# Second layer of a two-block model on one core: where pairs of expert rows stand among the query columns and the head norms

## What is computed

```python
k, v = shared_kv(x)                       # 16 heads of 64, k is rms-normed per head
q = rmsnorm((h @ w_q).heads) * 64**-0.5   # the head norm of the query rows
z = q @ k.T                               # per block of 128 tokens, strictly causal
a = exp(log_sigmoid(z) + sums of -softplus(z) over the keys between)
x = x + g1 * ((a @ v) @ w_out)
h = modulate(rmsnorm(x))                  # then the expert layer:
s = (h @ w_q) against 2 x 128 sub-keys, 8 heads
expert = 16 best of the sums of the 16 best of each half, per head
act = gelu(<peer_u[expert], h>)           # 8 x 16 = 128 experts for each token
x = x + g2 * sum((softmax(scores) * act) * peer_v[expert])
```

## Time and profile before

| | |
|---|---|
| median of 3 runs | 2526.04 us (2524.95 to 2527.66) |
| the profiled execution, its own time | 2526.39 us |
| its span | 2524.7 us |
| PE busy | 2032.2 us (80%) |
| DVE busy | 1719.8 us (68%) |
| ACT busy | 955.0 us (38%) |
| POOL busy | 658.8 us (26%) |
| moved by DMA | 823.98 MB, of these 595.97 MB by POOL's gathers |

### The profile page before, as it was taken

The page is one execution under the profiler, slowest core; times in us unless marked ns, Lnnn a source line. Parts: engine busy times, 40 slices in busy tenths (PEclk is TensorE's granted clock), DMA queues, the critical chain, the costliest instruction groups (busy, mean ns, idle before and its releaser), DMA issues.

```text
span 2524.7 us, 33890 instructions
## 1 busy us (share of the span) xinstructions
PE 2032.2 (80%) x12150; PEld 1384.9 (55%) x12150; DVE 1719.8 (68%) x3454; ACT 955.0 (38%) x2101; POOL 658.8 (26%) x631
## 2 busy tenths in 40 slices
PE   8999999999999999997665587777577778556555
PEld 7999899899989979874321123243122325211111
DVE  5687787768778867677588555558754757776544
ACT  4434533444544345432332224423223732322222
POOL 0000001000000100024445433344432335444442
PEclk9999999999999999999887798899788889887767
DMA  7545577674547763279999999999999999999998
GB/s 304 212 167 209 182 277 283 240 262 161 202 172 277 268 256 142 84 319 388 422 421 422 419 423 422 403 421 421 412 404 401 421 410 383 421 422 421 422 421 337
DMA packets 110947, 823.98 MB, mean 326 GB/s; under 512 B 14432, under 2 KB 15344, under 8 KB 31040
## 3 DMA queue, kind: packets, MB, share of 16 engines
q0 software_dynamic: 90000, 595.97, 57.8%
q1 hardware_dynamic: 20784, 225.89, 23.3%
HBM read 820.76 MB, written 1.05 MB: 326 GB/s over the span
## 4 chain that ended last, share of the span: by engine, by line
PE 47%; DMA 27%; DVE 11%; ACT 5%; issue 4%; POOL 2%; DVEq 2%; ACTq 1%; SPq 0%; POOLq 0%
DMA ring_b<-in_peer_uv,eidx 17%; PE pd L647 14%; PE pa L647 10%; PE pr L1269 9%; PE pr L647 7%; DMA wring<-in_peer_uv,eidx 6%; DVE wring_r L1971 2%; DVE ring_b L2672 2%; DMA ring_c<-in_peer_uv,eidx 1%; DVE wring L2672 1%; PE pa L1387 1%; ACT junk L1719 1%; POOL ring_b L1915 1%; PE pd L1292 1%; PE pa L1292 1%
## 5 line engine op out<-in xcount | busy, mean ns | idle before, releaser
L1269 PE MATMUL pr<-ring_b,junk 128*64 128x512 f32 x880 | 288.6, 765 | 156.5 <-ACT junk L1719 155.8
L1269 PE MATMUL pr<-wring,junk 128*64 128x512 f32 x840 | 269.4, 748 | 171.1 <-ACT junk L1719 170.6
L1915 POOL DMA_INDIRECT ring_b<-in_peer_uv,eidx x220 | 252.9, 1150 | 532.8 <-PE pr L1269 302.4
L2672 DVE CUSTOM_DVE_ANT_0 ring_b<-ring_b,hrow 128x1024 f32<-128x1024 f32 x220 | 267.9, 1224 | 180.9 <-DMA ring_b<-in_peer_uv,eidx 174.2
L2672 DVE CUSTOM_DVE_ANT_0 wring<-wring,hrow 128x1024 f32<-128x1024 f32 x210 | 255.4, 1223 | 187.8 <-DMA wring<-in_peer_uv,eidx 181.7
L1915 POOL DMA_INDIRECT wring<-in_peer_uv,eidx x210 | 247.8, 1180 | 332.6 <-PE pr L1269 277.3
L1709 ACT ACTIVATE gel<-dots 128x2 f32<-128x2 f32 x255 | 51.8, 203 | 654.4 <-DVE dots L2672 650.7
L1899 POOL DMA_DIRECT2D aring<-in_ada_rows x112 | 60.2, 538 | 840.9 <-DVE adal L2066 787.3
L1269 PEld LDWEIGHTS pr<-ring_b,junk 128*64 128x64 f32 x880 | 69.3, 165 | 350.8 <-ACT junk L1719 242.6
L1269 PEld LDWEIGHTS pr<-wring,junk 128*64 128x64 f32 x840 | 64.1, 159 | 345.6 <-ACT junk L1719 243.5
L1971 DVE TENSOR_TENSOR wring_r<-wring,wtop 128x2048 fp32r<-128x2048 f32 x76 | 171.7, 2261 | 54.7 <-ACT wtop L1431 52.4
(11 more groups left out here) (441 smaller groups left out, 4566.4 us busy)
## 6 DMA issues: line engine op xcount, KB each, us to landing
wring<-in_w_mix SPq DMA_DIRECT2D x38, 2048.0 KB, 8.8
aring<-in_ada_rows POOLq DMA_DIRECT2D x112, 512.0 KB, 5.1
wring<-in_w_ffn SPq DMA_DIRECT2D x22, 2048.0 KB, 8.3
wring<-in_w_lstm SPq DMA_DIRECT2D x12, 2048.0 KB, 7.7
wring<-in_w_stick SPq DMA_DIRECT2D x12, 2048.0 KB, 11.7
wring<-in_w_back SPq DMA_DIRECT2D x8, 2048.0 KB, 8.1
ring_c<-in_w_stick SPq DMA_DIRECT2D x5, 2048.0 KB, 12.1
wring<-in_w_back SPq DMA_DIRECT2D x4, 1536.0 KB, 6.9
```

Of the source, the lines that this page charges most:

```text
L1269: m = nc.tensor.matmul(pr[half][side, :], diag[:, p % DIAGS, :], row(p)[:, D + half * 512:D + (half + 1) * 512], start=p in FIRST_OF_SIDE, ...
L1915: pool.indirect_dma_start(out=row(q), out_offset=None, in_=ins["peer_uv"], in_offset=bass.IndirectOffsetOnAxis(ap=eidx[:, tt % NT, CHOSEN[ ...
L2672: m = nc.vector.tensor_tensor_reduce(out=row(q)[:, 0:D], in0=row(q)[:, 0:D], in1=hrow[:, q // PICKS % NT, SIDE[q], :], scale=1.0, scalar=0 ...
```

## The change

For the second layer:

- PE: all of the pair `heads` (picks 28 to 31) now stands between the transposes of the key rows and the wait for the query rows. Before, picks 28 and 29 stood behind the transposes of the query rows.
- DVE: `picks(tt, at["heads"])` stands ahead of the wait for the query rows, and so picks 30 and 31 ahead of their head norm. Before, they stood behind it.
- ACT: the gelus of that pair stand between the copies of the transposed key rows and those of the query rows.
- PE and ACT, query slots 0 and 1: a pair stands behind the second of four columns, and one behind the fourth, where before only one stood behind the slot. They no longer stay a pair behind. Slots 0 and 1 have 4 picks each (before 3 each for t = 0, 2 each for t = 1), and `keys` has 2 for both.
- The plan for t = 1: 98 picks ahead of the choice instead of 94, and 20 spread over it instead of 23.

```diff
 def plan_of(t):
-    out, q, step = ((3, 3, 48), (2, 2, 23))[t]
+    out, q, step = ((3, 4, 48), (2, 4, 20))[t]
 ...
-                   + [(("q", j), q) for j in range(2)] + [("keys", 4 - 2 * t)] + choice("choose", step, 2 - t))
+                   + [(("q", j), q) for j in range(2)] + [("keys", 2)] + choice("choose", step, 2 - t))
# PE
                 tile_columns(bank_a, pa_full, krow)
+                weighted(tt, at["heads"], False)
                 pe.wait_ge(sqk_ready, 2 * t + 2)
                 tile_columns(bank_a, pa_full, qrow)
-                weighted(tt, at["heads"])
 ...
-                    late_queries(j)
-                    weighted(tt, at["q", j])
+                    late_queries(j, lambda c: c == 1 and weighted(tt, at["q", j] - 2, False))
+                    weighted(tt, at["q", j], False)
                     late_keys(j)
# ACT
                 for dst in (skT[:, :, cut], sqT(t)):
                     for half in range(2):
                         nc.scalar.copy(...)
+                    gelus(tt, at["heads"])
                 act.drain().then_inc(sT_ready, 1)
-                gelus(tt, at["heads"])
 ...
                 for j in range(2):
+                    gelus(tt, at["q", j] - 2)
                     late_query(j)
                     gelus(tt, at["q", j])
                     late_key(j)
# DVE
                 heads_normed(krow, 0, 1.0)
-                picks(tt, at["in", 5])
+                picks(tt, at["heads"])
                 dve.wait_ge(srow_ready, 3 * t + 3)
                 heads_normed(qrow, 1, SB_DIM ** -0.5)
-                picks(tt, at["heads"])
```

## The result

The changed kernel takes 2536.18 us (median of 6, 2533.74 to 2536.89), the kernel before 2525.83 us beside it (6 runs, 2524.95 to 2527.66). The ratio is 1.0039 with a 95% interval of 1.0026 to 1.0052: 10 us slower, by 7 to 13. The forecast was 2530.5 us with a range up to 2537, so the time lies near its upper end. That end was rival C's; the forecast's own range ended at 2534.5 and is missed. The direction held, but the query slots lost where the sum had them gain.

The account below looks back on a forecast made before the run. Gathers bound the second part, so empty DMA time counts. Terms -4.2 + 0 + 5.3 + 3.4 = +4.5 us gave a forecast median of 2530.5 us; own range 2526.5 to 2534.5, wider range 2518 to 2537.

Parts of the forecast that it names:

- rival C: Query slots, t = 1: late choice, ring runs dry inside it, POOL waits over 5 us; 2534.7 to 2535.7 us; chance 0.20.
- What bounds the kernel: Second part of the kernel: gathers set the pace, so every microsecond with empty DMA engines counts; three holes, 1620, 1940, 2100.
- Head norms, when they begin: Query rows' head norms wait for picks 30 and 31, still in flight: 10.0 us late at t = 0, 8.1 at t = 1.
- The variant with equal bytes for both queues: Head norms: if queue turns meant equal bytes, pick 31 lands about 5 us sooner; t = 0 norm 5 us late, not 10.
- What the delay costs, t = 1: Behind the late head norm of t = 1: next gather 15.6 us later for 10.0 us of work; +5.3 us, bounds -3.0 to +8.1.
- 36 to 39 go out by 1940: Credit at t = 1: pairs multiplied in PE's idle 10.18 us let four more gathers go out, 10.0 us of DMA work.
- t = 0: +3.4: Late head norm of t = 0: core begins 7 us late, catches up part, output product 3.4 us late; bounds 0 to +7.
- so that this passes through whole: End of the t = 0 step: behind the output product is a hole with no stock, so all 3.4 us count.
- Query slots, t = 1: Pairs moved into slots 0 and 1 fill the hole at 2103 to 2113, 5.3 us; -4.2 us, bounds -5.3 to +3.
- begins some 3 to 4 rows behind and ends 4 to 5 behind: Choice of t = 1: DVE's lag behind the landed rows, of ten places, as 20 picks take about 53 us.
- close to the point at which POOL runs out, so I give 1.1 us back: Choice of t = 1: allowance for the ring nearly running out, turning the hole's -5.3 us into -4.2.
- Query slots, t = 0: Same moves in the first tile's slots, with no hole to fill in 1660:1680: 0 us, between -1 and +1.

Follow-up runs that it names:

- the control: The kernel before, unchanged, run again as an experiment of its own: +0.5 us (-1.8 to +2.8).
- e5_early_pair: Kernel before, its plan kept; second tile's slots 0 and 1 multiply both picks behind column 1, factors given ahead of the query copy: +4.3 us (1.8 to 6.6).
- e10_lagged_pair: Kernel before; on PE alone, second tile's slots 0 and 1, the same pair moved from behind column 3 to behind column 1: +0.5 us (-2.0 to +3.0).
- e12: Kernel before with the head norms' part of the change for the first tile (t = 0) only: +1.0 us (-1.3 to +3.3).
- e11_dve_only: Kernel before with only DVE's order changed, both tiles: dots of picks 30 and 31 ahead of the query norm: +10.6 us (6.8 to 14.2).
- e2: Kernel before with the query-slot part and the plan of the change alone, heads as before: +3.0 us (0.8 to 5.6).
- e4: Kernel before with the slots' part, but the pair behind column 4 of slots 0 and 1 put behind the sub-key products: +1.0 us (-1.0 to +3.3).
- e6: Kernel before with the changed plan, all of a slot's picks behind column 3 and no longer a pair behind: +1.3 us (-1.3 to +3.8).
- e3_pe_pair_only: Kernel before, but PE multiplies picks 28 and 29 ahead of the wait for the query rows; DVE and ACT unchanged: +0.5 us (-1.8 to +2.8).
- e1_heads_only: Kernel before with the heads' part of the change alone, on PE, ACT and DVE, both tiles: +8.6 us (5.6 to 11.9).
- e8_heads_t1: Kernel before with the head norms' part of the change for the second tile (t = 1) only: +7.8 us (5.1 to 10.9).

## Why the prediction was right or wrong

**What bounds the kernel.** Right: from 1900 on the empty time separates the kernels with an edit in the stage from those without, 10.0 to 11.0 us against 0.8 to 5.5 in 1900-2080, and 7.9 to 11.5 against 5.2 to 6.7 in 2080-2240. But the size of a hole in one profile was taken for a property of the kernel, and at 1940:1960 it was not. The first hole varies too: 1600:1660 misses 2.8 us in the profile of before, 1.6 in the control, 2.6 in e5_early_pair and 0.4 in e10_lagged_pair, none of which touches the first tile. Nor is one profile's span a measure: between 1100 and 1540, where nothing was edited, the same count gives 5.4 us in the profile of before and up to 15.7 (e12) in the others.

**Head norms, when they begin.** Right at both tiles: 10.0 us late forecast and 9.9 measured for t = 0, 8.1 and 9.0 for t = 1. The reason, that picks 30 and 31 are still in flight, is shown by the DMA waits on their dots and by e11_dve_only. The variant with equal bytes for both queues (5 us late at t = 0) fell. In the earlier trace rows the packets are nearly equal, 38 and 33, and the bytes are not, so the prediction's "the turns are unequal" reads more into these rows than they show.

**What the delay costs, t = 1: +5.3, measured +7.8.** The mechanism held, the size was low, at the edge of the interval. The failed piece is the credit, "36 to 39 go out by 1940". Picks 36 and 37 went out by 1934.1 in the kernel after. 38 and 39 went out at 1942.5 and 1944.4, since pair 30, 31 could be multiplied only at 1938.04, behind the dots that themselves had waited for the DMA, and ScalarE's factors. Its credit fell into a time in which the control's engines were nearly full anyway. Pick 40, forecast for 1956, went out at 1958.71, in a profile that ran 4.9 us behind at pick 32. Counted from pick 32 it goes out 41.1 us on, where the forecast had 43.2. In the kernel before that was 37.1, but in the control only 32.1: against its own profile the delay was put 2 us too high, and against the control it is 9 us.

**t = 0: +3.4, measured +1.0.** That the core catches up part of the delay was right. Counted from the dot of pick 29, the output product begins 79.2 us on in both profiles of the kernel before, 82.2 in the kernel after and 84.2 in e12_heads_t0: 3.0 and 5.1 us late, where 3.4 was forecast. (The clock time alone says little: 1623.26 in the kernel after, 1622.82 in the control.) What failed is the end of the step, "so that this passes through whole". In the kernel after 1620:1640 runs at 424, and the account by stage has about half of the loss back by 1900. The two errors in the heads' part cancel, by luck: +8.7 forecast, +8.6 measured.

**Query slots, t = 1: -4.2, measured +3.0.** This is the step that failed, and rival C came nearer. Its total, 2534.7 to 2535.7, is the measured time within the interval, but it is made of +5.3, +3.4 and 0 to +1, where the parts measured +7.8, +1.0 and +3.0, and its sign, a wait of POOL of over 5 us inside the choice, is not there (4.0 at most). The ring ran dry a little inside the choice (379 at 2140:2160) and mostly behind it (322 at 2180:2200).

The hole went, as forecast. The keys of slot 1 were put 11 us late; the choice came 13.7 us late. DVE's place in the ring was forecast rightly, "begins some 3 to 4 rows behind and ends 4 to 5 behind". It had read every row as it landed by 2122.3 and then stood 9.07 us, in which rows go on landing at 2.49 us each; none of the 20 dots inside the choice waits for the DMA; and behind the choice it reads five rows back to back, 118 to 122, where the kernel before reads two. The kernel before, the first dot behind the choice that waits again (pick 119):

```profile
2172.91 1.22 DVE L2672 CUSTOM_DVE_ANT_0 ring_c<-ring_c,hrow 128x1024 f32<-128x1024 f32 x1 [1.39 <-DMA ring_c<-in_peer_uv,eidx]
```

The kernel after, picks 118, 122 and 123 on DVE, the pair 114, 115 on PE, and the gather of pick 124:

```profile
2182.70 1.23 DVE L2673 CUSTOM_DVE_ANT_0 ring_c<-ring_c,hrow 128x1024 f32<-128x1024 f32 x1
...
2187.28 1.22 DVE L2673 CUSTOM_DVE_ANT_0 ring_b<-ring_b,hrow 128x1024 f32<-128x1024 f32 x1
2188.75 1.23 DVE L2673 CUSTOM_DVE_ANT_0 ring_b<-ring_b,hrow 128x1024 f32<-128x1024 f32 x1 [0.24 <-DMA ring_b<-in_peer_uv,eidx]
```

```profile
2183.05 3.68 PE L1269 MATMUL pr<-ring_b,junk 128*64 128x512 f32 x8 [5.04 <-ACT junk L1719]
```

```profile
2187.54 1.78 POOL L1916 DMA_INDIRECT ring_b<-in_peer_uv,eidx  x1 [8.22 <-PE pr L1269]
```

What failed is the price put on this, "close to the point at which POOL runs out, so I give 1.1 us back". By the rate, 2140:2220 lacks 9.0 us in the kernel after and nothing in the two profiles of the kernel before: a debit of 9.0 against the 5.6 that filling 2100:2120 brought. The ten places were counted as if DVE alone held them. At the end of the choice picks 114 to 117 had been read but were not yet multiplied, beside the rows that DVE had still to read. When gather 124 went out at last, 91.1 us behind the first column, only pick 123 had still to land; in the two profiles of the kernel before it goes out 86.2 and 89.6 us behind it, with four and three rows still in flight. TensorE waits there for factors that ScalarE gives only behind its copy of slot 3's scores, and that copy is late with everything else behind the slots: 81.7 us behind the first column in the kernel after (2178.05 - 2096.40) and 67.2 in the control (2155.31 - 2088.12). That these two together make the debit is read from the traces; no run moved one without the other.

An account that would have given the sign from the forecast's own numbers: four picks more ahead of the choice are 4 x 2.49 = 10.0 us of transfers brought forward, paid for with 11.3 us of lateness, so +1.3 and not -4.2. For the six kernels that touch these slots, lateness less transfers brought forward gives 3.7 (after), 5.2 (e2), 2.4 (e4), 5.4 (e5), 2.9 (e6) and 3.4 (e10) us, 3.8 on average. The empty time of 2080-2240 above the mean of the eight others, 5.8, is 3.0, 5.7, 4.7, 2.1, 2.6 and 4.7, also 3.8. But by the clock five of the six cost +3.0, +1.0, +4.3, +1.3 and +0.5, 2.0 on average (the sixth, the kernel after, has the heads' part too), so this account gives the sign and about twice the size. It was also formed after the fact.

**Query slots, t = 0: 0.** Measured 0.0.

What stays open: which of the slot arrangements is the least bad, since their medians differ by less than they can be told apart; and why e5_early_pair costs 3 us more than e6_plan_only by the clock and 0.5 us less by its empty time. No arrangement was found that beats the kernel before; e3_pe_pair_only and e10_lagged_pair only equal it. Both in one kernel was not tried.

## What to carry to other kernels

Before work is moved ahead of a wait, look whether its own operand has landed by then. Two dots of 1.2 us ahead of each of two norms cost 10 us here, because free work behind the norm became a DMA wait in front of it.

A hole in a transfer is worth filling only if what fills it doesn't make the step late that feeds the next stock of transfers. Set the lateness of everything behind, in order, against the transfers brought forward, in the same unit. And count a place of the ring as taken until the last engine has freed it, not until the first has read it.

And profile the unchanged kernel a second time before pricing a hole: of the three holes here one was nearly gone in the second profile (0.6 us in place of 3.0) and another was about half as large.

## What the runs showed of the hardware

TensorE's clock has two levels, 2.4 GHz (1.00) and 1.2 GHz (0.50). In the three kernels with the whole heads' part at t = 1 the clock granted in 1940:1960 was 0.51 (after), 0.50 (e1_heads_only) and 0.50 (e8_heads_t1). In the kernel after it stood at 0.50 from 1936 to 1956 in every stretch of 4 us. Before it fell and while it was low, PE idled 6.04 us ahead of the pair at 1938.04 and 2.95 us ahead of the transposes, and was busy for 12.56 us of the 20. The kernel before has one idle stretch of 10.18 us and was low too, but for a shorter time: 0.53 and 0.50 in 1928:1936, 0.69 in 1936:1940 and 1.00 in 1940:1944. In the control, with 5.45 us idle, only 1936:1940 is at 0.50.

Rows at either level: the 16 score products (L1325, L1328 in e8_heads_t1) behind the transposes took 3.09 us in each of the three kernels and 1.71 in the control. The 16 matmuls behind them, ahead of pick 40, took 6.33, 5.01 and 6.59 us in the three, 5.24 in the kernel before and 5.35 in the control and in e11_dve_only, so for these the price is not the same in every profile. The sum had no term for the clock; on the chain to pick 40 it is some 1 to 3 us, an estimate from these rows.
